# Long convolutions of a block kernel: filters undivided and made between the projections, the inverse norm in the short convolution's weights, the modulation rows early

## The reference

```python
def hyena_filters(...):
    feats = concat([t_norm, cos(fw), -sin(fw)])
    h = sin(fr[0] * (feats @ f_w1 + f_b1))
    h = sin(fr[1] * (h @ f_w2 + f_b2))
    h = sin(fr[2] * (h @ f_w3 + f_b3))
    h = (h @ f_w4).reshape(L, 2, HYENA_ORDER, D_MODEL) * window
    h = h * rsqrt(sum(h * h, axis=(0, 1), keepdims=True) + EPS)
    return h[:, 0], h[:, 1]

def bidir_long_conv(u, hf, hb, skip):        # kernel: as products of spectra
    kfull = concat([hf, zeros_like(hf[:1]), hb[:0:-1]])
    return irfft(rfft(u, 2L) * rfft(kfull, 2L))[:L] + u * skip

def hyena_mixer(h, ...):
    x1, x2, v = split(short_conv(h @ w_in, conv_w, conv_b), 3)   # 3 taps and a bias
    y = v
    for n, gate in enumerate((x1, x2)):
        y = gate * bidir_long_conv(y, hf[:, n], hb[:, n], skip[n])
    return y @ w_out

m = silu(c) @ w_mod[i] + b_mod[i]            # sh1, sc1, g1, sh2, sc2, g2
x = x + g1 * mixer(rmsnorm(x) * (1 + sc1) + sh1)
x = x + g2 * (square(relu(modulate(x) @ w1)) @ w2)
```

## Time and profile before

| | us |
|---|---|
| three runs: median (lowest to highest) | 2618.68 (2607.84 to 2622.43) |
| the profiled execution's own time | 2618.72 |
| its span | 2616.9 |
| PE busy | 2379.7 (91%) |
| DVE busy | 1922.8 (73%) |
| ACT busy | 1345.3 (51%) |

### The profile page before, as it was taken

How to read it: one execution, slowest core, us unless ns; L and a number is a source line. 1 busy time by engine, 2 the same in 40 slices (tenths; PEclk the granted TensorE clock), 3 DMA queues, 4 the chain that set the end, 5 groups by cost and what they waited for, 6 DMA issues and landing times.

```text
span 2616.9 us, 29868 instructions
## 1 busy us (share of the span) xinstructions
PE 2379.7 (91%) x11058; PEld 1744.7 (67%) x11058; DVE 1922.8 (73%) x2327; ACT 1345.3 (51%) x1481; POOL 23.5 (1%) x44
## 2 busy tenths in 40 slices
PE   7998999999998979999999989998999568876998
PEld 6556777777773548777777765574987226733887
DVE  2737999999993558999999988656665443469764
ACT  3226888888882327888888861353332011102332
POOL 0000000000000000000000000000000000000000
PEclk9988999999998988999999999998999679988999
DMA  9214988888993315989998885512575401307370
GB/s 327 101 71 175 387 358 358 358 358 357 368 369 127 129 63 198 368 367 366 372 374 361 360 327 169 207 54 91 197 271 182 171 32 65 129 8 262 133 278 27
DMA packets 116248, 606.80 MB, mean 232 GB/s; under 512 B 5288, under 2 KB 8416, under 8 KB 91388
## 3 DMA queue, kind: packets, MB, share of 16 engines
q1 hardware_dynamic: 111536, 588.83, 58.0%
q0 software_dynamic: 4624, 16.76, 1.8%
HBM read 604.51 MB, written 1.05 MB: 231 GB/s over the span
## 4 chain that ended last, share of the span: by engine, by line
PE 56%; DVE 22%; issue 13%; ACT 9%; DVEq 1%; DMA 0%; POOL 0%; SPq 0%; ACTq 0%
PE bank L930 10%; DVE slab_parts L2501 8%; ACT high L1772 5%; PE bank L942 4%; PE bank L1231 4%; PE bank L1183 3%; PE bank L1047 3%; PE bank L1210 3%; PE bank L1464 2%; PE bank L1466 2%; PE bank L1465 2%; PE bank L1172 2%; PE bank L1445 2%; PE bank L1447 2%; PE bank L1446 2%
## 5 line engine op out<-in xcount | busy, mean ns | idle before, releaser
L2501 DVE TENSOR_TENSOR slab_parts<-ring,high 128x2048 fp32r<-128x2048 f32 x384 | 862.3, 2288 | 39.0 <-ACT high L1772 34.5
L1772 ACT ACTIVATE high<-ring 128x2048 fp32r<-128x2048 f32 x384 | 728.6, 1914 | 44.0 <-PE bank L1183 35.9
L1183 PE MATMUL bank<-high,xT_parts 128*128 128x512 f32 x1024 | 294.7, 410 | 17.8 <-DVE slab_parts L2501 14.1
L1183 PE MATMUL bank<-slab_parts,xT_parts 128*128 128x512 f32 x1024 | 279.3, 394 | 0.0
L1616 ACT ACTIVATE arena<-bank 128x512 f32<-128x512 f32 (+4 forms) x166 | 91.7, 584 | 355.6 <-PE bank L942 95.6
L930 PE MATMUL bank<-ring,xT 128*128 128x512 f32 (+3 forms) x576 | 238.2, 575 | 9.9 <-ACT xT L1616 5.0
L1183 PEld LDWEIGHTS bank<-high,xT_parts 128*128 128x128 f32 x1024 | 184.5, 190 | 78.7 <-DVE slab_parts L2501 38.4
L1183 PEld LDWEIGHTS bank<-slab_parts,xT_parts 128*128 128x128 f32 x1024 | 193.9, 189 | 45.7
L1778 ACT ACTIVATE arena<-bank 64x512 f32<-64x512 f32 (+2 forms) x352 | 184.7, 534 | 61.7 <-PE bank L1210 51.7
L930 PEld LDWEIGHTS bank<-ring,xT 128*128 128x128 f32 x576 | 110.7, 193 | 134.0 <-issue 123.3
L1636 ACT ACTIVATE high<-ring 128x2048 fp32r<-128x2048 f32 x64 | 121.9, 1912 | 123.5 <-PE bank L1447 82.2
(11 more groups left out here) (373 smaller groups left out, 3606.1 us busy)
## 6 DMA issues: line engine op xcount, KB each, us to landing
ring<-in_moe_w_gate SPq DMA_DIRECT2D x64, 2048.0 KB, 8.5
ring<-in_moe_w_up SPq DMA_DIRECT2D x64, 2048.0 KB, 9.3
ring<-in_moe_w_down SPq DMA_DIRECT2D x64, 2048.0 KB, 9.2
ring<-in_mlp_w SPq DMA_DIRECT2D x32, 2048.0 KB, 13.2
ring<-in_w_mod SPq DMA_DIRECT2D x24, 2048.0 KB, 8.1
ring<-in_even_w_in SPq DMA_DIRECT2D x7, 2048.0 KB, 21.3
ring<-in_odd_w_in SPq DMA_DIRECT2D x6, 2048.0 KB, 10.8
ring<-in_h_w_in SPq DMA_DIRECT2D x6, 2048.0 KB, 8.9
```

Of the source, the lines that this page charges most:

```text
L1183: last = mm(dst[:, :], seated2[:, 4 * half + k, e], part_[:, k, :], start=(half == a == k == 0), stop=(half == a == 1 and k == 3))
L1772: act_fn(hi, weight_half(layer, name, half), ACT.Copy).then_inc(sem(f"high{layer}"), 1)
L2501: v.tensor_tensor(low, w, hi.bitcast(F32), ALU.subtract).then_inc(sem(f"low{layer}"), 1)
```

## The change

Four parts.

1. **The MLP of layer 0 takes in `mod1.pre1`.** `MLP_MODS` replaces `GATE_SUMS`: in layer 0 the two parts of `gate2` come at steps 2 and 3 and the four of `mod1.pre1` at steps 4 to 7. Each has its slab in the ring, its `multiply_c`, its `sum_up` and its addition. `widen_c` and `c_product` go for layer 1. The MLP of layer 1 keeps steps 3 and 5.
2. **The filter's three small layers** (`filter_layer`, `filter_angle`, `filter_sin`) move into the first projections of layer 0's attention, between `mla_cq` and `gqa_q`.
3. **The mixer's first half.** The filter matmuls stand between the transposition and the first projection slabs, which are taken in the order v, v, x1, x1, x2, x2. The filters stay undivided. Their squares go to ACT, eight of 128x1024, each summed by PE into one row of a bank. The root is taken of that row. Its reciprocal, after a transposition to columns, multiplies the weights and bias of the short convolution for x1 and x2. The skip times the root is added to the filter's first tap, so that the separate skip multiplication and addition go. `mod1.gate1` and `mod1.pre2` are multiplied and collected between the projections, as rows of `mod_rows`.
4. **The long convolutions go in halves of 512 columns**, so that the way back of one half can start before the spectra of the other are done. Behind them, gate and shift are spread from `mod_rows`, and the residual sum follows the output projection at once.

```diff
-GATE_SUMS = (3, 5)
+MLP_MODS = ({2: ("mod0.gate2", 0), 3: ("mod0.gate2", 1), 4: ("mod1.pre1", 0), 5: ("mod1.pre1", 1),
+             6: ("mod1.pre1", 2), 7: ("mod1.pre1", 3)}, {3: ("mod1.gate2", 0), 5: ("mod1.gate2", 1)})
+HYENA_ORDER = (4, 5, 0, 1, 2, 3)
...
+            if j + 2 in mods:
+                self.vector_slabs(mods[j + 2][0], 1)
...
             slab_in(K["mla_cq"][0])
             project(U["mla_cq"], K["mla_cq"][0], 384, tokens)
+            filter_layer(0)
             turn("turn.ctx", ctx_u.rearrange("p (t d) -> p t d", t=NT), 5)
             turned("turn.ctx")
+            filter_layer(1)
             for name, n in (("mla_ckv", 288), ("gqa_q", 512), ("gqa_kv", 256)):
+                if name == "gqa_q":
+                    filter_layer(2)
...
+            pe.wait_ge(sem("filter_h"), 3)
+            slab_in(K["filter_w4"][0])
+            filters(0, range(4))
+            turn("turn.n1_1", u3, 7)
+            turned("turn.n1_1")
+            hyena_in(0, 0)
+            filters(0, range(4, 8))
+            filters(1, range(8))
+            hyena_in(0, 1)
+            filter_sums(0)
+            filter_sums(1)
+            hyena_in(1, 0)
+            hyena_in(1, 1)
...
+            hyena_turn(0)
+            collect(U["mods1"][0], MODS1[0])
+            pe.wait_ge(sem("dft_loaded"), 16)
+            filter_dft(0)
+            filter_dft(1)
+            for i in range(2, 6):
+                for j in range(2):
+                    hyena_in(i, j)
+                hyena_turn(i - 1)
+                if i == 4:
+                    collect(U["mods1"][1], MODS1[1])
+            hyena_turn(5)
+            collect(U["mods1"][2], MODS1[2])
...
+                for half in range(2):
+                    pe.wait_ge(sem("spectrum_ready"), 4 * n + 2 * (half + 1))
...
             for j, u in enumerate(U["mla_cq"]):
                 copy_out(u, z_cq[:, j * 384:(j + 1) * 384], banks[u.bank][:, 0:384])
+            filter_sin(0)
             turn("turn.ctx", ctxT)
+            filter_sin(1)
             root(384, 2)
...
             multiply_c("mod0.gate1", 0)
+            filter_angle(0)
+            filter_angle(1)
             for u in U["mla_cq"]:
...
-                link(v.reciprocal(f_norm, f_norm))
-
-                link(v.tensor_scalar(h44[:, 1, 0], h44[:, 1, 0], col("not_first"), None, ALU.mult))
...
+            multiply_c("mod1.gate1", 0)
+            convolve(0)
+            multiply_c("mod1.gate1", 1)
+            dma_done(dve, "skip_loaded")
...
+            link(v.tensor_tensor(skip_row, skip_row, std_row, ALU.mult))
+            for n in range(2):
+                sums = f_sum[n].rearrange("p (t d) -> p t d", t=NT)
+                link(v.tensor_tensor(sums, filt[n][:, 0], filt[n][:, 1], ALU.add))
+                link(v.tensor_tensor(filt[n][:, 1], filt[n][:, 0], filt[n][:, 1], ALU.subtract))
+                tell(v.tensor_tensor(f_sum[n][0:1, 0:D], filt[n][0:1, 0, 0], skip_row[:, n * D:(n + 1) * D], ALU.add),
+                     "filter_sums")
...
-                    link(v.tensor_tensor(y, y, skip[:, half * 512:(half + 1) * 512], ALU.mult))
-                    drain(v.tensor_tensor(y, y, banks[u.bank][:, :], ALU.add), u)
-                    tell(v.tensor_tensor(y, y, hy_x[n][:, cs], ALU.mult), "hyena_y")
...
+                    drain(v.tensor_tensor(hy_x[2][:, cs], banks[u.bank][:, :], hy_x[n][:, cs], ALU.mult), u)
```

More of the change, by code:

```diff
@@ L288, in make_plan @@
         p.take(f"idft{n}", 4)
-    p.vector_slabs("mod1.gate1", 2)
+    p.take("mod1.gate1", 2)
+    p.take("mod1.pre2", 2)
     p.take("turn.hyena_out", 4)
@@ L293, in make_plan @@
         if i == 0:
-            for k in range(2):
-                p.sum_up("mod1.gate1", k)
-    p.vector_slabs("mod1.pre2", 4)
-    for k in range(4):
-        p.sum_up("mod1.pre2", k)
+            p.take("mod1.pre2", 2)
     p.take("turn.n2_1", 4)
-    p.mlp("mlp1", "mod1.gate2")
+    p.mlp(1)
     return p
@@ L1569, in _ @@
-            pe.wait_ge(sem("hyena_y"), 8)
-            turn("turn.hyena_out", hy_x[2].rearrange("p (t d) -> p t d", t=NT))
+                for half in range(2):
+                    if n == 1:
+                        for u in U["idft0"][2 * half:2 * half + 2]:
+                            drained(pe, u)
+                    for j in range(4):
+                        u = U[f"dft{n}"][4 * half + j]
+                        ft, kind = j // 2, j % 2
+                        claim(u)
+                        table = (cosT, sinT)[kind]
+                        for k in range(NT):
+                            last = mm(banks[u.bank][:, :], table[:, k, ft * P:(ft + 1) * P],
+                                      hy_x[2][:, k * D + half * 512:k * D + (half + 1) * 512], start=(k == 0), stop=(k == 1))
+                        tell(last, u)
@@ new lines, in _ @@
+                for half in range(2):
+                    pe.wait_ge(sem("spectrum_ready"), 4 * n + 2 * (half + 1))
+                    for tile in range(NT):
+                        u = U[f"idft{n}"][2 * half + tile]
+                        claim(u)
+                        for i, (table, src) in enumerate(((icos, y_re), (isin, y_im))):
+                            for k in range(NT):
+                                last = mm(banks[u.bank][:, :], table[:, k, tile * P:(tile + 1) * P],
+                                          src[:, k * D + half * 512:k * D + (half + 1) * 512],
+                                          start=(i == 0 and k == 0), stop=(i == 1 and k == 1))
+                        tell(last, u)
@@ new lines, in _ @@
+            for name in ("mod1.gate1", "mod1.pre2"):
+                for k in range(2):
+                    spread(U[name][k], name, k, U["mods1"][2])
+            for j in (0, 2, 1, 3):
+                u, half = U["turn.hyena_out"][j], j % 2
+                for done in U["idft1"][2 * half:2 * half + 2]:
+                    drained(pe, done)
+                claim(u)
+                for i in range(4):
+                    c0 = (j // 2) * D + (4 * half + i) * P
+                    last = nc.tensor.transpose(banks[u.bank][:, i * P:(i + 1) * P], hy_x[2][:, c0:c0 + P], ident)
+                tell(last, u)
@@ new lines, in filter_std, with spectrum_out @@
+            def filter_std(n):
+                for half, u in enumerate(U[f"filter_norm{n}"]):
+                    c0 = n * D + half * 512
+                    full(act, u)
+                    if n == half == 0:
+                        full(act, U["filter1"][-1])
+                    act_fn(std_row[:, c0:c0 + 512], banks[u.bank][0:1, :], ACT.Sqrt, bias=eps_col[0:1])\
+                        .then_inc(bank_drained[u.bank], 1)
+            def spectrum_out(n):
+                dst = spectra[:, 4096 * n:4096 * (n + 1)].rearrange("p (k f d) -> p k f d", k=2, f=NT)
+                for j, u in enumerate(U[f"filter_dft{n}"]):
+                    kind, half, ft = j // 4, j // 2 % 2, j % 2
+                    if kind == 1 and ft == 0:
+                        full(act, U[f"filter_dft{n}"][j + 1])
+                    copy_out(u, dst[:, kind, ft, half * 512:(half + 1) * 512], banks[u.bank][:, :])
@@ L1970, in _ @@
+            x_out(5)
+            copies("mod1.gate1", gate_h)
+            copies("mod1.pre2", shift_h, units=2)
             turn("turn.hyena_out", xT3)
```

470 lines of the change are left out of this document (251 added, 219 removed).

## The result

The changed kernel took 2581.07 us (median of 4 runs, 2578.81 to 2584.59), the kernel before 2616.27 beside it (2607.84 to 2622.43): a ratio of 0.9869, with a 95% interval of 0.9837 to 0.9900. It is 35 us faster, where 72 were forecast, and 1 us above the top of the range of 2520 to 2580. The direction was right and half of the gain is missing.

A forecast was written before the change was run, and what follows sets the result against it. In the mixer no engine is full and engines wait for each other; layer 0's MLP is PE alone. 2618.7 + 14.3 + 20.4 + 19.1 - 126.1 = 2546 us, range 2520 to 2580.

The forecast's parts named there:

- Filter's small layers: Layer 0's attention: PE resumes 11.7 us late behind the context's transposition; with slow clock and third layer +14.3 us, bounds 10 to 17.5.
- Start of layer 0's MLP: Second w1 slab waits for a sum_up and lands late, delaying the MLP's first matmul: +20.4 us, bounds 19 and 24.
- Four parts in that MLP: Layer 0's MLP: four more sum_ups, and PE waits in steps 3 to 6 for late loads: +19.1 us, bounds 3.4 to 28.
- The rival of shared engines: Layer 0's MLP: loads share the engines instead of landing in turn, so slabs land later: 29 us more, 2575; chance 15%.
- The mixer: From layer 0's MLP end to the next MLP's first matmul: 283.1 us against 409.2, so -126.1 us, bounds 110 to 138.
- The sums of squares: Mixer: 16 matmuls with a single output row, taken at 0.87 us each, 14.0 in all; below 7, above 28.
- the columns of the root: Mixer, behind the sums of squares: columns of the root, a transposition and a collect, 4.7 us.
- Layer 1's MLP: The MLP behind the mixer, in its old order: expected unchanged at 185 us.
- What is delayed there is lost whole: Three touched places ahead of the mixer: all on the critical path, so each delay counts in full.
- the first place and the second: The filter's small layers in layer 0's attention (+14.3 us) and the start of layer 0's MLP (+20.4 us).
- the clock among its rivals: Mixer: TensorE stays at the low clock, 1.2 GHz throughout, adding 236 us: 2782; chance 3%.
- the first term: The filter's small layers in layer 0's attention, forecast to cost +14.3 us.

The follow-up runs named there:

- fillers in the pauses: Changed kernel plus nine matmuls of 128 columns with unread results, four and five in the two pauses ahead of gqa's heads: 2541.11 us, ratio 0.9728.
- with the Sins late: Changed kernel with each Sin of the filter's small layers one place later, the first behind ACT's copies of the context's transposition: median 2559.15 us, runs 2529.33 to 2567.46.
- with four matmuls: Changed kernel plus four matmuls of 128 columns (0.9 us) on PE ahead of the first logits of mla's heads: 2542.92 us, ratio 0.9728.
- the burst's kernel: Changed kernel plus 24 matmuls of 128 columns ahead of the fifth logits of gqa's heads: 2553.64 us, ratio 0.9741.

## Why the prediction was right and wrong

- **Filter's small layers, forecast +14.3.** Right: 14.8 in the profile, 13.5 between kernels on one chip. The projection came 12.2 later than in before, seen from the projection ahead of it, and the slow clock added 1.8 (2.1 forecast).
- **Start of layer 0's MLP, forecast +20.4.** Right: 20.7. The slab was issued behind the sum_up and landed in 9.07 (8.5 taken).
- **Four parts in that MLP, forecast +19.1.** Right with a small surplus: 17.6. The waits are in steps 3 to 6 as forecast, 10.9 in all instead of 12.7. The rival of shared engines (29 more) is refuted by the same rows, with waits below the forecast's and a slab that landed in 9.07.
- **The mixer, forecast -126.1.** Right: -121.9. To the first projection 11.9 (12.3), up to the long convolutions 166.6 (164.5), from there to the output projection 64.1 (63.8), the rest 44.6 (42.5). The sums of squares (32 records, 14.1 us busy) took 0.88 us per matmul where 0.87 were put in, so here a single output row costs as much as 128. The largest error inside is at the columns of the root: with the transposition and the collect behind them 9.7 us instead of 4.7. Behind the 32 records of one column the level was down, without a wait: the transposition took 1.97 (1.04 later in the mixer) and the collect 3.61. Half of the output projection, too, took 15.70 instead of 13.97.
- **Layer 1's MLP.** 183.4, unchanged but for 1.4.

The four terms together were forecast at -72.3 and measure 14.8 + 20.7 + 17.6 - 121.9 = -68.8: 3.5 us apart. The step that failed is the sentence that carried the sum, "What is delayed there is lost whole". It took a stretch that is moved to last as long as before, and so put the attention between the first place and the second at nothing; it measures +34.3, all of it in and behind gqa's heads, by the clock. The forecast had put the clock among its rivals, but only in the new mixer, and held against it that "each row after a wait shows about 3 us lost, not more". Those rows were of stretches with long matmuls, where the level comes back. They didn't even show the same loss each time: the 13.97 that the forecast took from "a continuous stretch" stands behind a wait of 0.99 us, and a group as long took 16.37 behind one of 0.88. In gqa's heads no row of before showed a fall, since in the profiled run there was none; and there a fall is not taken back. The changed kernel reaches the two pauses ahead of gqa's heads at a moment at which the level falls: 34.3 us, against a miss of 35.

Shown: the fall is where the time went (trace); fillers in the pauses prevent it (16 runs of 16, in four kernels, at 2544 and below as their other edits say, with four traces); with shifts of 0.9 to 2.3 us, of work or of idleness, none of 12 runs bears its size (three traces); the unchanged kernel falls in 8 of 8; gqa's heads keep the level that they find in both directions, mla's didn't keep the low one. The kernel before may not be free of it either: three of its runs have the size. Open: what makes a moment a bad one. From the start of the projection ahead of the context's transposition (1602.80 in before, 1604.23 after) to gqa's first logits it is 135.1 us in the kernel before (3 of 44 runs bear the size of a loss), 135.7 with the Sins late (4 of 5), 149.8 in the changed kernel (8 of 8), and 0.9 more than that with four matmuls (none of 4). The three runs of 44 are all of one chip. No rule in this distance alone can be read from these runs, and I forecast none. So it is shown that a shift of under a microsecond undoes the fall, but that the 14.8 us of the first term are what brought it on is only argued. The Trainium skill (TensorE: Matmul & The Clock Gate, "HAM oscillation") tells of groups that begin at the low clock because long waits stand between them, and advises to order the loop so that the matmuls run on without such waits. With work in both pauses the clock is 1.00 here too. But gqa's loop has no wait in it and still stays low for 72 us, so here the measurement decides.

## What to carry to other kernels

When a change shifts a stretch of PE's work in time, even by a microsecond, ask of each stretch behind it whether it would climb back from the low clock, not only whether it fell before: short matmuls and transpositions in an unbroken row may keep a low level for as long as they last. A few dummy matmuls in the short pauses ahead cost nothing here (49.23 us with and without) and kept the full level in 16 runs of 16. And a load whose place in a ring is held by a late reader should be issued behind the loads that are needed sooner, as everything behind it in the queue pays for its wait.

## What the runs showed of the hardware that was not expected

- PE without a gap at a granted clock of 0.51, from gqa's first logits to their last, 72.18 us with the 0.76 ahead of the spreads.
- The same two pauses (0.82 and 1.11 us, with a transposition of 2.81 between them) brought the level down at one moment of the program (8 of 8 runs, two traces and a third in the burst's kernel), and at moments 0.9 to 2.3 us later in none of 12 (three traces); with some 14 us taken away upstream the times went from 2529 to 2567 in 5 runs, with one trace, of the fastest.
- After a hole of 4.57 us in mla's heads the level came back some 14 us later in the midst of unchanged work; after one of 3.87 us in gqa's it didn't within 33.
